# One added wait on GpSimd: table six of eight waits for the third down step of the second feed-forward

## The reference

```python
# first block: mixer, then a feed-forward with squared relu, then a gated embedding
h = h + jnp.square(jax.nn.relu(z @ w_up[l])) @ w_down[l]
...
# second block
x = x + 0.5 * rms_norm_2(swiglu(h, ffn1_w_in[l], ffn1_w_out[l]), ffn1_post_g[l])
h = rms_norm_2(x, mix_pre_g[l])
proj = h @ w_mix_in[l]
attn = dilated_attention(q, k, v)
ssm = s5_mixer(u, a_re[l], a_im[l], log_dt[l], b_re[l], b_im[l], c_re[l], c_im[l], ...)
x = x + rms_norm_2(mixed, mix_post_g[l])
x = x + 0.5 * rms_norm_2(swiglu(h, ffn2_w_in[l], ffn2_w_out[l]), ffn2_post_g[l])
```

## Time and profile before

| | us |
|---|---|
| median of 3 runs | 2832.86 |
| lowest and highest | 2830.86, 2833.11 |
| profiled execution | 2837.0 |
| its span, first to last instruction | 2835.2 |
| TensorE busy | 2771.5 (98%) |
| VectorE busy | 1994.8 (70%) |
| ScalarE busy | 1224.0 (43%) |
| GpSimd busy | 535.2 (19%) |
| mean granted TensorE clock | 0.992 |

### The profile page before, as it was taken

The page is one execution under the profiler, slowest core; times in us unless marked ns, Lnnn a source line. Parts: engine busy times, 40 slices in busy tenths (PEclk is TensorE's granted clock), DMA queues, the critical chain, the costliest instruction groups (busy, mean ns, idle before and its releaser), DMA issues.

```text
span 2835.2 us, 35454 instructions
## 1 busy us (share of the span) xinstructions
PE 2771.5 (98%) x13040; PEld 2268.9 (80%) x13040; DVE 1994.8 (70%) x2946; ACT 1224.0 (43%) x1894; POOL 535.2 (19%) x1023
## 2 busy tenths in 40 slices
PE   8999999999999999999989999999999999999998
PEld 7778888878887878888877778887788888888786
DVE  5754977787675579888878682336656977777758
ACT  6534555544344364333324353136655433332434
POOL 0001000000000001899989600011101000000000
PEclk9999999999999999999999999999999999999999
DMA  3123344498572123333368642212124123323864
GB/s 139 45 93 123 123 150 144 148 338 277 181 259 75 48 87 112 126 136 126 137 219 310 226 162 75 83 67 79 55 82 163 64 104 112 112 99 136 299 246 164
DMA packets 132460, 405.50 MB, mean 143 GB/s; under 512 B 14928, under 2 KB 15696, under 8 KB 129984
## 3 DMA queue, kind: packets, MB, share of 16 engines
q1 hardware_dynamic: 114224, 329.82, 33.6%
q0 software_dynamic: 18064, 73.41, 7.0%
HBM read 296.88 MB, written 105.12 MB: 142 GB/s over the span
## 4 chain that ended last, share of the span: by engine, by line
PE 86%; DVE 7%; DMA 3%; ACT 1%; issue 1%; SPq 0%; DVEq 0%; ACTq 0%
PE ps L127 26%; PE ps L129 26%; PE ps L128 26%; PE ps L2658 1%; PE ps L2673 1%; PE ps L2632 1%; DMA late_raw_b<-hid 1%; PE ps L281 1%; DVE mixed_b L1512 1%; DMA near_raw<-hid 1%; DMA hid<-pieces_b 1%; PE ps L2308 1%; PE ps L352 0%; DVE up_slots L1086 0%; PE ps L2341 0%
## 5 line engine op out<-in xcount | busy, mean ns | idle before, releaser
L1079 ACT ACTIVATE up_slots<-weight_sums 128x512 fp32r<-128x512 f32 x216 | 136.2, 631 | 304.3 <-PE ps L129 282.2
L127 PE MATMUL ps<-region_a,up_slots 128*128 128x512 f32 x640 | 250.4, 391 | 2.3 <-DVE late_pieces L1159 0.9
L127 PE MATMUL ps<-mixed_b 128*128 128x512 f32 x584 | 232.2, 398 | 18.0 <-DVE mixed_b L1512 10.4
L129 PE MATMUL ps<-region_a,up_slots 128*128 128x512 f32 x640 | 249.1, 389 | 0.0
L128 PE MATMUL ps<-region_a,up_slots 128*128 128x512 f32 x640 | 249.0, 389 | 0.0
L128 PE MATMUL ps<-mixed_b 128*128 128x512 f32 x584 | 230.0, 394 | 0.0
L129 PE MATMUL ps<-mixed_b 128*128 128x512 f32 x584 | 229.8, 393 | 0.0
L127 PE MATMUL ps<-region_a,region_b 128*128 128x512 f32 x448 | 181.4, 405 | 4.8 <-DVE region_b L122 3.9
L129 PE MATMUL ps<-region_a,region_b 128*128 128x512 f32 x448 | 175.5, 392 | 0.0
L128 PE MATMUL ps<-region_a,region_b 128*128 128x512 f32 x448 | 175.0, 391 | 0.0
L1086 DVE TENSOR_TENSOR up_slots<-weight_sums,up_slots 128x512 fp32r<-128x512 f32 x216 | 158.3, 733 | 7.2 <-ACT up_slots L1079 7.1
(11 more groups left out here) (580 smaller groups left out, 7017.9 us busy)
## 6 DMA issues: line engine op xcount, KB each, us to landing
raw<-feed SPq DMA_DIRECT2D x98, 512.0 KB, 4.4
far_raw_b<-feed SPq DMA_DIRECT2D x65, 512.0 KB, 4.3
raw<-stream SPq DMA_DIRECT2D x56, 512.0 KB, 3.5
xn<-hid SPq DMA_DIRECT2D x46, 512.0 KB, 6.1
hid<-pieces_b SPq DMA_DIRECT2D x33, 512.0 KB, 2.9
far_raw_a<-feed SPq DMA_DIRECT2D x33, 512.0 KB, 4.1
x_mid<-acc POOLq DMA_DIRECT2D x32, 512.0 KB, 3.3
ssm_row<-ssm_mid POOLq DMA_DIRECT2D x8, 1632.0 KB, 7.5
```

The costliest lines, as they stand in the source:

```text
L127: nc.tensor.matmul(psum, lhs(0), rhs(0), start=first, stop=False)
L129: return nc.tensor.matmul(psum, lhs(1), rhs(0), start=False, stop=last)
L1079: nc.scalar.activation(up_slot(F, i)[:, 0, :], F.weight(p, q), ACT.Copy).then_inc(F.sem["hi"], 1)
```

## The change

GpSimd gets one more wait, ahead of table 6 (b = 5): it goes on only once TensorE has finished the third step of the down stage of `ffn1`.

```diff
@@ -3190,6 +3190,8 @@
                     pool.dma_start(gb[:, 0, :], rows[2, :, :]).then_inc(gb_in[0], 16)
                 if b >= NB - 2:
                     old_rows_again(pool, n_mix2, 0, range(4 * (b - NB + 2), 4 * (b - NB + 3)))
+                if b == 5:
+                    pool.wait_ge(*ffn1.down_done(2))
                 ssm_make_pool(pool, b)
             keep_new_rows(pool, n_mix2)
             pool.wait_ge(*n_mix2.at("res", NT))
```

## The result

| | before | after |
|---|---|---|
| median, us | 2831.41 (6 runs) | 2843.78 (6 runs) |
| lowest and highest | 2827.46, 2833.11 | 2841.73, 2846.09 |
| profiled execution | 2837.0 | 2843.0 |
| its span | 2835.2 | 2841.2 |

The ratio of the times is 1.0043, with a 95% interval from 1.0033 to 1.0053: the change makes the kernel slower by 12.4 us. The profiled executions differ by 6.0 us.

The account below looks back on a forecast made before the run. TensorE, busy 98% of the span, was taken to bound the kernel. The 10 us gained are waited away; table 8's 8.5 us lateness less 4, plus low clock, gives +5: 2838 on the median, range 2823 to 2847, forecast's own 2833 to 2844.

Parts of the forecast that it names:

- The release: End of GpSimd's added wait on the third down step: 1468.5 instead of 1424.1, so table 6 comes 44 us later.
- Table 6: GpSimd's sixth table, now fully in the down stage's heavy stretch: 67 us, done at 1536.
- Hand-over: GpSimd's store and reloads between tables: 7 us between tables 6 and 7, 5.6 us between 7 and 8.
- Table 7: GpSimd's seventh table: starts at 1543, enters the light stretch at about 1560, done at 1594.
- Table 8: GpSimd's last table: starts at 1600, done 1666, landed 1670; VectorE passes its wait there 8.5 us later than before.
- The last quarter's pace: Table 8 beside VectorE's last down-stage quarter: 1.89 times slower, 86 us for a table; other bound 52.8 us.
- The gain at the entry: Start of the down stage without GpSimd: 6.9 us of TensorE waits and about 3 of low clock, 10 us.
- VectorE's own slowing: VectorE slowed beside GpSimd before its wait for table 8: an estimated 5 us, reaching the wait at 1657.
- VectorE's idle: Ahead of the rows' third reciprocal, VectorE idles 8 to 15 us, released by a store to the tables' memory.
- What reaches the end: After VectorE's wait: 8.5 us late less 4 of slack and saved idle, with low clock +5 us.
- The base: Starting time for the +5 us: profiled execution 2837.0 gives 2842, the median of 2832.86 gives 2838.
- Strict turns: Rival: at the shared port each of table 8's 96 instructions waits out a subtraction; +15 us, 2848; chance 0.10.

Follow-up runs that it names:

- a silent table 6: Kernel before with gain row and all eight reloads ahead of table 8 and table 6's computing left out: 2820.49 us, ratio 0.996.
- the spread reloads: Kernel before with gain row and four reloads ahead of table 8, four reloads behind it, no pause; run twice: 2826.62 and 2826.61 us.
- an empty table 8: Changed kernel with table 8's computing left out, its load, stores and all waits kept: 2822.14 us, ratio 0.9954.
- the reloads put in: Changed kernel with gain row and first four reloads right behind the pause, ahead of table 6: 2852.39 us, ratio 1.0069.
- the reloads taken away: Kernel before with gain row and all eight reloads issued ahead of table 8, no pause: 2826.40 us, ratio 0.9967.

## Why the prediction was right, and where its sizes were off

The sign and the mechanism were forecast: table 8 late for VectorE's wait, and the whole entry gain waited away. The size was not: +5 us was forecast and the medians are 12.4 apart. The predicted 2838 is 5.8 us under the median of 2843.8, which lies inside the range and at the very upper end of the forecast's own range, which went to 2844. That it does is owed in part to the width of the ranges. A loss over the 5.7 us bound had been given 0.36, less than the 0.46 for a smaller one. (By the parts listed, faster comes to 0.16 and same to 0.48; the text has 0.18 and 0.46.) Step by step:

- **The release.** Taken at 1468.5, measured 1469.04.
- **Table 6.** Taken at 67 us, it took 80.0. It is the largest error of the sum, 13 us. The reason given, that table 7 took 70.0 while VectorE was catching up, points the wrong way: in the kernel before, VectorE had idled in that stretch (58.56 of 70 us), in the kernel after it was busy for 58.57 of 60. A faster TensorE keeps VectorE fuller, and so GpSimd slower.
- **Hand-over.** 7 taken, 4.8 measured, and the next 5.6 taken, 4.2 measured.
- **Table 7.** Started at 1554.6 instead of 1543, it lay almost wholly in the light stretch and took 46.4 us where 51 were taken. That gave back 5.
- **Table 8.** The two errors left its start at 1605.2, 5 us late; taken from 1600 to 1666, it ran from 1605.2 to 1666.25, in 61 us, because VectorE stood still from 1650 and not only from 1657. The landing was 3.3 us (3.7 taken), and VectorE passed its wait at 1669.6 (1670 taken). The number is right by errors that cancel.
- **The last quarter's pace.** Taken 86 us for a table, on the nearest row. A table's first 71 instructions took 49.7 us in 1605 to 1655, with VectorE at work beside them until 1650, against 30.2 in the light stretch (1554.61 to 1584.79). That is 1.65 times, against 1.89 taken, the first 5 us of it still light. The up stage's bound of 52.8 us for a table was far off.
- **The gain at the entry.** Taken at 10 us, it was 14.0 in the traces (VectorE's line 190 starts at 1622.29 instead of 1636.27). Of it 10.0 us are waits (16.4 to 6.4) and the rest goes with the clock, 0.96 against 1.00 in the window from 1425 to 1600. The wait at the change to the last quarter, left out of the gain, shrank from 4.8 to 2.6 us. The split was also wrong: the working put the gain to undisturbed subtractions and to table 6's stores, with the reloads named only in passing. The reloads are over half of it by the counts (31 of 58 matmuls) and about half by the medians (5 to 9 us, and 6 to 7 for a silent table 6). Delaying one store gave nothing beyond the noise; what both cost in the entry isn't shown.
- **VectorE's own slowing.** 5 us were taken. It reached the wait at 1649.97, 11.5 us earlier than in the kernel before: of a lead of 14.0 it lost 2.5 beside GpSimd.
- **VectorE's idle.** 8 to 15 us were forecast, 19.6 measured: the wait ended when foretold, and VectorE was there 7 us sooner. TensorE's idle was put at about 1665; it ran dry behind the matmul of 1652.94, 16 us ahead of the 1669.5 at which it needs that row in the kernel before. The working doesn't say how it came to 1665; with its own gain of 10 us the row was needed at about 1660.
- **What reaches the end.** The sum had 8.5 - 4 and half a microsecond of clock. Measured: the wait ends 8.1 us later than in the kernel before (1669.60 against 1661.50), the idle behind it shrinks so that line 1512 starts 6.5 us later (1670.46 against 1663.98), 3.2 us of slack go, and the low clock costs 2.4: 5.7, against a measured 5.8. Of these only the clock was undersized.
- **The base.** The forecast took the profiled execution's difference, +5, for that of the medians. The profiles do differ by 6.0, the medians by 12.4. The profiled execution of the kernel before, 2837.0, is 3.9 us above the slowest of its six runs in the table, while that of the kernel after lies among its runs. The two traces alone don't explain the other 6 us, but the experiments point at the trace of the kernel before. From the end of TensorE's first wait of over 1 us in the stage to the first transposes it takes 217.0 us (1457.28 to 1674.25). The two runs of the spread reloads take 205.0 and 206.9, 12.0 and 10.1 less, and by the medians they are only 5.6 and 5.1 us faster. For every changed kernel but one the median is worse than this stretch would have it, by 0.5 to 6.6 us, and by 6.2 for the kernel after. So that execution probably lost some us more in this stage than is usual. That would bring the 6.0 us between the profiles towards the 12.4 between the medians, and the entry gain of 14.0 us and the 58 matmuls would be upper values. It isn't shown, since there is no second trace of the kernel before; against it stands that the kernel with an empty table 8 is 13.8 us faster by the medians, close to its 59 matmuls more (13.4 us), though the kernel before had a higher median beside it (2835.91). The kernel before had a median of 2832.18 and 2831.71 beside the other experiments; the kernel after was timed against 2831.41 alone.

**The rule on the shared port.** The prediction said that GpSimd wasn't stopped beside VectorE. Instruction by instruction, that was too weak a reading. GpSimd's timeline in the kernel after, where VectorE's wide subtractions begin at 1610.57, and then where VectorE is silent:

```profile
1610.29 0.25 POOL L2209 TENSOR_TENSOR made_osc<-tmp_p 128x32 f32<-128x32 f32 x1
1610.62 1.32 POOL L2204 TENSOR_TENSOR tmp_p<-made_osc,st 128x64 f32<-128x64 f32 x1
1611.90 1.27 POOL L2205 TENSOR_TENSOR tmp_p<-made_osc,st 128x64 f32<-128x64 f32 x1
1613.13 0.74 POOL L2206 TENSOR_TENSOR tmp_p<-made_osc,st 128x64 f32<-128x64 f32 x1
...
1664.73 0.30 POOL L2206 TENSOR_TENSOR tmp_p<-made_out,st 128x64 f32<-128x64 f32 x1
```

The same shape takes 0.30 us alone and up to 1.32 beside VectorE: about 1 us more, near one subtraction of 1.22 us. This agrees with the rule of the Trainium skill, "SBUF — State Buffer", section "Who interferes with whom", that the second of two such instructions fully blocks until the first is finished. Strict turns was too dear as a rival for another reason: it added 1.2 us to each of 96 instructions on top of the 45.5 us of a table that had already run beside a VectorE busy for 27.34 of 46 us, and not every instruction meets one (the one at 1613.13 took 0.74 us).

## What to carry to other kernels

Before a wait is put ahead of work that runs in the background, add up when the last of that work must be done, and price its pace by how busy the engine beside it will be there after the change, not before it. When a pause gains something, ask which of the things behind it did: here moving eight reload transfers, without any wait, gave 2826.40 us (ratio 0.9967 [0.9955, 0.9979], and 0.9983 or 0.9984 where half of them went behind table 8), less than either kernel of the case. Look for slack in both directions: a gain made ahead of a fixed meeting point is lost if the partner comes no earlier. And take the size of a change from medians of several runs: one trace of each kernel can be several us off.

## What the runs showed of the hardware

- Adding to an accumulator with one operand in PSUM did not disturb GpSimd here, subtracting with both operands in SBUF did. From 1607 to 1610.5 us VectorE runs lines 1577 and 1579 (acc <- acc, ps; 0.68 us each) and GpSimd's instructions take 0.20 to 0.25 us; with line 1512 from 1610.57 they take up to 1.32. VectorE's timeline of the kernel after there:

```profile
1609.96 0.69 DVE L1579 TENSOR_TENSOR acc<-acc,ps 128x512 f32<-128x512 f32 x1
1610.57 2.45 DVE L1512 TENSOR_TENSOR mixed_b<-late_raw_b,mixed_b 128x1024 fp32r<-128x1024 f32 x2
...
1625.26 3.18 DVE L1512 TENSOR_TENSOR mixed_b<-late_raw_b,mixed_b 128x1024 fp32r<-128x1024 f32 x2
```

- The cost is one-sided but not wholly. The two subtractions take 2.36 us undisturbed, 2.45 beside GpSimd's instructions of 128x64, and 3.18 beside those of 128x256, which themselves take 1.6 instead of 0.6 us.
- Four reloads (2 MB, issued in 2.86 us) and the gain row (0.5 MB) on GpSimd's own queue slow the loads of another queue enough to cost TensorE 5 to 7 us, both ways (728 against 750 matmuls with them put in, 723 against 692 with them taken away). The rows of `hid` issued from 1440 to 1510 us by line 1700 show it: their slowest landing takes 17.1 us with the reloads put in and 9.7 in the kernel after, and half of them take over 8.4 us in the kernel before and 6.7 with the reloads taken away.
- Behind an idle of 19.5 us TensorE starts again at a low clock: 0.63 is granted from 1670 to 1680 us, and 21 matmuls of 128x512 take 7.2 us where 4.8 would do.
